# Weight buffers at 64 and 192 bytes within 512 from the streaming operand, in a two-block sequence model on one core

## The reference

```python
proj = rms_norm(x, pre_mix_norm) @ w_in                 # 1024 x 6688
o_a = gdn_chunked(...); o_s = ssd_chunked(...)          # from slices of proj, after conv and silu
x = x + rms_norm(concatenate([o_a, o_s]) @ w_out, post_mix_norm)
u = causal_dwconv(rms_norm(x, pre_ffn_norm) @ w_up, ffn_conv_w, ffn_conv_b)
gate, up = split(u, 2)
x = x + rms_norm((silu(gate) * up) @ w_down, post_ffn_norm)
for layer in range(2):                                  # second block
    x = x + (even_mixer, odd_mixer)[layer](rms_norm_2(x, norm[layer]))
    x = x + conv_ffn(rms_norm_2(x, ffn_norm[layer]))    # (silu(a) * g) @ w_down
```

## Time and profile before

| | |
|---|---|
| median of 3 runs | 2159.37 us (2159.14 to 2168.34) |
| profiled execution, span | 2157.8 us |
| PE busy | 2109.7 us, 98% |
| PE weight loads | 1698.0 us |
| DVE / ACT / POOL busy | 1213.1 / 906.3 / 325.6 us |
| matmuls | 9776 |
| DMA | 188.96 MB, mean 88 GB/s |

### The profile page before, as it was taken

The page is one execution under the profiler, slowest core; times in us unless marked ns, Lnnn a source line. Parts: engine busy times, 40 slices in busy tenths (PEclk is TensorE's granted clock), DMA queues, the critical chain, the costliest instruction groups (busy, mean ns, idle before and its releaser), DMA issues.

```text
span 2157.8 us, 26841 instructions
## 1 busy us (share of the span) xinstructions
PE 2109.7 (98%) x9776; PEld 1698.0 (79%) x9776; DVE 1213.1 (56%) x1663; ACT 906.3 (42%) x1282; POOL 325.6 (15%) x266
## 2 busy tenths in 40 slices
PE   6999999999999999999999999999999999999999
PEld 5778888878868888877766888888878878888887
DVE  5898755765366665226544566653354465666522
ACT  6883445434254444224564444442242354444311
POOL 0002121220122222001302122210000011222100
PEclk9999999999999999999999999999999999999999
DMA  7323322122323233221111333232222122323321
GB/s 234 93 77 92 86 74 69 59 69 69 101 65 97 94 94 120 94 86 59 59 40 50 97 94 94 95 116 96 80 77 88 51 78 88 98 97 97 114 94 66
DMA packets 81481, 188.96 MB, mean 88 GB/s; under 512 B 19824, under 2 KB 40432, under 8 KB 81392
## 3 DMA queue, kind: packets, MB, share of 16 engines
q1 hardware_dynamic: 81392, 187.75, 27.6%
HBM read 178.28 MB, written 9.44 MB: 87 GB/s over the span
## 4 chain that ended last, share of the span: by engine, by line
PE 92%; DVE 4%; ACT 2%; issue 1%; DMA 0%; POOL 0%; SPq 0%; ACTq 0%; DVEq 0%; POOLq 0%
PE acc L253 23%; PE acc L255 23%; PE acc L254 23%; PE bank L1726 1%; PE bank L1245 1%; PE bank L229 1%; PE bank L230 1%; PE bank L231 1%; PE acc L2634 1%; PE acc L2633 1%; PE acc L2632 1%; PE bank L2017 1%; PE bank L253 1%; PE bank L255 1%; PE bank L254 1%
## 5 line engine op out<-in xcount | busy, mean ns | idle before, releaser
L253 PE MATMUL acc<-HH,whi 128*128 128x512 f32 x1600 | 642.1, 401 | 7.1 <-DVE wlo L191 4.5
L255 PE MATMUL acc<-HH,wlo 128*128 128x512 f32 x1600 | 624.4, 390 | 0.0
L254 PE MATMUL acc<-HL,whi 128*128 128x512 f32 x1600 | 623.5, 390 | 0.0
L185 ACT ACTIVATE whi<-raw 128x1024 fp32r<-128x1024 f32 (+1 forms) x293 | 324.2, 1108 | 573.5 <-PE acc L255 543.4
L191 DVE TENSOR_TENSOR wlo<-raw,whi 128x1024 fp32r<-128x1024 f32 (+1 forms) x293 | 400.9, 1369 | 287.8 <-ACT whi L185 287.8
L253 PEld LDWEIGHTS acc<-HH,whi 128*128 128x128 f32 x1600 | 301.1, 188 | 74.1 <-DVE wlo L191 11.0
L255 PEld LDWEIGHTS acc<-HH,wlo 128*128 128x128 f32 x1600 | 300.5, 188 | 64.0
L254 PEld LDWEIGHTS acc<-HL,whi 128*128 128x128 f32 x1600 | 301.1, 188 | 62.0 <-issue 4.1
L253 PE MATMUL acc<-FH,whi 128*128 128x512 f32 x528 | 208.9, 396 | 0.0
L255 PE MATMUL acc<-FH,wlo 128*128 128x512 f32 x528 | 208.6, 395 | 0.0
L254 PE MATMUL acc<-FL,whi 128*128 128x512 f32 x528 | 208.5, 395 | 0.0
(11 more groups left out here) (394 smaller groups left out, 2673.1 us busy)
## 6 DMA issues: line engine op xcount, KB each, us to landing
raw<-w SPq DMA_DIRECT2D x257, 512.0 KB, 3.5
raw<-w SPq DMA_DIRECT2D x48, 704.0 KB, 4.0
X<-x SPq DMA_DIRECT2D x4, 512.0 KB, 5.2
x_dram<-small SPq DMA_DIRECT2D x8, 256.0 KB, 4.4
xt_dram<-small SPq DMA_DIRECT2D x8, 256.0 KB, 3.6
a_dram<-l_am SPq DMA_DIRECT2D x8, 256.0 KB, 3.7
l_xt<-xt_dram SPq DMA_DIRECT2D x8, 256.0 KB, 3.5
l_x<-x_dram SPq DMA_DIRECT2D x8, 256.0 KB, 3.3
```

The lines of the kernel that those rows point to most:

```text
L185: nc.scalar.activation(hi[:, 0:kt * P], raw[u % RAW][:, 0:kt * P], ACT.Copy).then_inc(w_hi_ready, 1)
L253: nc.tensor.matmul(a[:, :], wh, tile(hi, k), start=start and k == 0, stop=False)
L254: nc.tensor.matmul(a[:, :], wh, tile(lo, k), start=False, stop=False)
L255: last = nc.tensor.matmul(a[:, :], wl, tile(hi, k), start=False, stop=stop and k == kt - 1)
```

## The change

whi0 and wlo0 begin at a place that is 64 bytes, whi1 and wlo1 at one that is 192 bytes behind that of HH modulo 512. Before, all four began at HH's place modulo 512. Within a pair wlo follows whi by 5,632 bytes, a multiple of 512, so it has the same place. FREE is taken at 128 behind HH's place modulo 512; before it came out there by the rounding to 128. FREE is 512 bytes further up. To make room for that below the end, five tables (t_nbe, t_beta, t_neg, t_sum, t_negsum) go to columns 1024 to 1175 of raw0, of which the units of that stage fill only the first 1024, and l_ors follows t_exp. No instruction, wait or transfer is added, removed or moved.

```diff
+TILE_LINE = 512
+WEIGHTS_AT = (64, 192)
...
-        whi = [fixed(f"whi{j}", [P, HALF * P], F32R) for j in range(SPLIT)]
-        wlo = [fixed(f"wlo{j}", [P, HALF * P], F32R) for j in range(SPLIT)]
+        whi, wlo = [], []
+        for j, shift in enumerate(WEIGHTS_AT):
+            top[0] += (base_h + shift - top[0]) % TILE_LINE
+            whi.append(fixed(f"whi{j}", [P, HALF * P], F32R))
+            wlo.append(fixed(f"wlo{j}", [P, HALF * P], F32R))
...
-        FREE = (top[0] + LINE - 1) // LINE * LINE
+        FREE = top[0] + (base_h + LINE - top[0]) % TILE_LINE
...
-        t_soft, t_ld, t_exp, t_nbe, t_beta, t_neg, t_sum, t_negsum = (place(n, k, tab0 + 4 * o) for n, k, o in (
-            ("t_soft", 128, 0), ("t_ld", 96, 128), ("t_exp", 288, 224), ("t_nbe", 32, 512), ("t_beta", 32, 544),
-            ("t_neg", 24, 576), ("t_sum", 32, 600), ("t_negsum", 32, 632)))
+        t_soft, t_ld, t_exp = (place(n, k, tab0 + 4 * o) for n, k, o in (
+            ("t_soft", 128, 0), ("t_ld", 96, 128), ("t_exp", 288, 224)))
+        t_nbe, t_beta, t_neg, t_sum, t_negsum = (raw[0][:, KD * P + o:KD * P + o + k] for k, o in (
+            (32, 0), (32, 32), (24, 64), (32, 88), (32, 120)))
...
-        l_ors = place("l_ors", S, tab0 + (664 * 4 + LINE - 1) // LINE * LINE)
+        l_ors = place("l_ors", S, tab0 + 512 * 4)
```

## The result

The changed kernel takes 2181.22 us (median of 4 runs, 2178.57 to 2183.41) against 2163.86 for the kernel before in the same comparison: ratio 1.0078, 95% interval 1.0054 to 1.0101. It is slower by 17.4 us. I had forecast 2114 us. The measured time lies inside my range of 2070 to 2192 only because that range reached to the slower rival; it is on the other side of no change from the forecast.

What follows compares the result with a forecast made beforehand. PE, busy 98% of the span, was taken as the bound through its matmul steps. 2157.8 less 45.4 us from the new weight places, other terms about 0, plus 1.6 for the median: 2114 us, range 2070 to 2192.

Steps and rivals of the forecast that it cites:

- slower rival: HH and HL matmuls lose the best distance, 64 and 192 cost 233.3 ns: 32 us more, 2191 us; chance 0.22.
- My rival that the change does nothing: Something other than place separates the 227 and 233 ns steps of the split matmuls: 2159 us; chance 0.09.
- point 1: Weights at 64 and 192: all affected split matmuls step at 222 ns, saving 49.3 us, 45.4 on the chain.
- The floor of 214 ns: Least step thought possible for a full-rate matmul, half the 429 ns read for the f32 matmuls of L2498.
- The inference on 128-byte borders: Weight load and stream meet at 128-byte borders from distances that are multiples of 128, not from 64; basis for 222 ns.
- Half way: Split matmuls at 64 lie between distances 0 and 128, 230 ns for all: 9.5 us more, 2169 us; chance 0.17.
- deciding point: Time rises once the HH step exceeds 226.7 ns by more than 2,160/5,304 of what FH gains.
- the weak step: The inference, seen in no row, that split matmuls at 64 and 192 avoid border meetings and step at 222 ns.
- Points 2 to 5: No new bound on DVE, ACT, POOL or DMA; weight splits, shifted small buffers and moved tables cost about nothing.
- point 5: Five tables in the tail of raw0, read by DVE and ACT with the same instructions: no cost.
- Point 4: par, cst, small move 192 bytes, FREE and all behind it 512; f32 matmuls 0 to 6 us, taken as 0.
- if the steps differ between pair 0 and pair 1: Sign in the changed timeline that one distance is good, the other not, and one value for both was wrong.

Runs made afterwards that it cites:

- w0_free128: The changed kernel with both weight pairs at 0 again, FREE at 128, five tables still moved: 2167.15 us against 2167.46 before, ratio 0.9991.
- w192_free128: The changed kernel with both weight pairs at 192, FREE at 128; 8.5 us against the kernel before at equal clock, its median is not given.

## Why the prediction was wrong

**What bounds the kernel** was right: PE's steps alone move the time. In every kernel run here the steps give the time to within 7 us by the medians and to about 2 us at equal clock, and the 92% for the chain served (18.3 us worked out, 17.4 measured).

**The reading that the distance counts** was right. It was drawn from 226.5, 233.3 and the 225 ns of L218, and the map confirms it with other engines idle. Here the page's rule that PE never waits (Trainium skill, "SBUF — State Buffer", "Who interferes with whom") does not cover what is measured: 6.7 ns a matmul hang on the place. My rival that the change does nothing, which had 0.09, is out by 1.0054.

**The step that failed is point 1, the value of 222 ns for distances that the trace did not have.** Measured were 233.3 at 64 and 229.0 at 192, in the kernel 231.9 and 231.6. Three parts of it were wrong.
- The floor of 214 ns was half of what I read as the f32 step. It took for granted that the split type streams as tightly as f32. At 512 columns it has 13.3 ns over its columns at best, so 226.7 is the floor and the earlier trace rows stood on it already. The row was misread besides: the eight records of L2498 are four matmuls (`ssd_sums` issues four), so a plain f32 matmul takes 858 ns, and 214 is half of a record and a quarter of a matmul. The page's gap formula (Trainium skill, "TensorE: Matmul & The Clock Gate", "Back-to-back issue gap") gives 216 ns. That section names no type; bf16 agrees with 215.8, the split type does not. The trace of before held a warning: of all its split matmuls not one of some 7,500 steps is under 224 ns (read from the starts), at whatever moment the weight load began, and 214 would have needed some.
- The inference on 128-byte borders had no row. The period is 256, so 0 and 128 were not two of a kind, and "multiples of 128" was the wrong class. A distance off those multiples bought nothing: 64 has 233.3, as 128 has.
- With the true floor, the range of the unknown step was 226.7 to 240, all of it on the slow side for HH. Then only FH and the others could gain, at most 2,160 x 6.6 x 0.92 = 13 us, and a change that moves HH off a distance known to be good to one that is not known could hardly pay. The edit that the trace supported was the reverse: to bring FREE to 0.

**Half way** (230 ns, 2169) and **slower** (233.3 for HH, 2191) stand on either side of the result. HH came to 231.9, three quarters of the way from 227.5 to 233.3. The slower rival is right for pair 0, in that 64 costs what 128 costs; why it does is open, since its picture of two reads that meet badly did not stand with 32 weight columns (231.7 ns). Its size (6.6 ns for both pairs) was too large by half, since 192 has a better rhythm. Its deciding point, HH's loss over 2,160/5,304 of FH's gain, was passed: 4.4 ns against 0.41 x 1.6. I gave the two 0.39 together and the forecast 0.52, on the strength of an argument that I had called the weak step myself.

**Points 2 to 5** held: no engine came to be the bound, L190 and L196 kept 1053 and 1319 ns, the f32 records are 429.2 ns apart at distances 0, 64 and 128, and w0_free128 bounds the tables, l_ors and the buffers' order (point 5) at -0.2 to 0.04%. Point 4 rests on w192_free128, which has the shifted par, cst, small and FREE and fits its split steps at equal clock (8.5 and 8.5 us). HH with first stayed (232.6 and 232.9; the 236 that I had read from five steps is at its high end). Of my signs, "if the steps differ between pair 0 and pair 1" was the one that came true.

## What to carry to other kernels

Where PE is the bound, read the step from start to start, and compare it between groups of the same shape: two values for one shape are a finding. Before a place, a size or an order is moved to a value that the trace doesn't have, map it in a kernel of its own; one short run gave all 40 distances and would have decided this case. Take a floor from the same type: half the step of another type is not a bound. Count records against the instructions of the program before a record's time is taken as that of an instruction. For this type at 128x512, begin weights and streamed tiles at the same place within 256 bytes.

## What the runs showed of the hardware

- The step of a split (fp32r) 128x512 matmul depends on the distance of its weights from the streamed operand with a period of 256 bytes: 226.7 ns at 0 and 16 bytes on either side, 229 to 235 elsewhere. bf16 (215.8) and f32 (429.2 for each of two records of a matmul) don't depend on it at 0, 64 and 128.
- At 256 streamed columns the order is another, 120.0 at 0 and 117.8 at 64; fewer weight columns don't shorten the step at distance 0 (231.7 with 32). So the best place holds for one shape.
- What the step has over N/2.4 GHz at distance 0 is 13.3 ns at 512, 384, 320 and 256 columns, 16.7 at 504 to 480 and 16.0 at 448: 504 columns take as long as 512. Between 192 and 128 columns it does not change (111.6 ns).
- Steps settle into rhythms (226, 229, 232; 231, 236; 233), and a distance can have two, 229 and 233.3 at 192; by the traces it looks as if the second is carried over from the unit before, which no run tested. What in PE or SBUF makes the period was not found.
- Runs of one kernel differ by up to 0.6% with the time at 1.2 GHz (kernel before, 38 runs: 2157.7 us at a mean clock of 0.998 to 2170.5 at 0.991); in the profiled executions of the kernel before and after most of that time lies in the first 650 us among the chains of small matmuls.
